# Attention of a streaming-encoder layer: unnormalised softmax with one buffer, against scaled probabilities of two key groups on two column halves

## The reference, cut to what matters

```
s = einsum('bcqhgd,bcshd->bchgqs', qc, kb) * (A_HEAD_DIM ** -0.5)
s = where(valid, s + bias, -1e30)
m = maximum(max(s, axis=-1), sink)
p = exp(s - m)
denom = sum(p, axis=-1) + exp(sink - m)
o = einsum('bchgqs,bcshd->bcqhgd', p / denom, vb)
...
mix = concatenate([y_a, y_b], axis=-1)      # y_a: attention, y_b: retention
x = x + mix @ w_out
```

## Time and profile before

| what | us |
|---|---|
| median of 3 runs (577.29 to 580.09) | 577.47 |
| the profiled execution | 576.34 |
| its span, first to last instruction | 574.2 |
| TensorE busy in it | 549.9 |
| VectorE, ScalarE, GpSimd busy | 423.5, 359.3, 116.7 |

### The profile page before, as it was taken

The page is one execution under the profiler, slowest core; times in us unless marked ns, Lnnn a source line. Parts: engine busy times, 40 slices in busy tenths (PEclk is TensorE's granted clock), DMA queues, the critical chain, the costliest instruction groups (busy, mean ns, idle before and its releaser), DMA issues.

```text
span 574.2 us, 8097 instructions
## 1 busy us (share of the span) xinstructions
PE 549.9 (96%) x2782; PEld 451.3 (79%) x2783; DVE 423.5 (74%) x572; ACT 359.3 (63%) x477; POOL 116.7 (20%) x102
## 2 busy tenths in 40 slices
PE   3999999999999999998999999999999999999992
PEld 3988878888878888876788888888888888888860
DVE  2664577454764843377988889888898888988887
ACT  4563554781134363335778887788877888778823
POOL 3350000000000000002443234432244323411100
PEclk9999999999999999999999999999999999999998
DMA  8989212203020236677999999999999999999173
GB/s 299 373 277 387 58 36 74 74 20 128 1 73 1 74 111 226 231 276 272 344 390 373 371 366 365 368 367 335 346 372 389 372 359 374 369 389 339 34 294 146
DMA packets 72044, 144.32 MB, mean 251 GB/s; under 512 B 3794, under 2 KB 13322, under 8 KB 71888
## 3 DMA queue, kind: packets, MB, share of 16 engines
q1 hardware_dynamic: 65936, 124.96, 61.7%
q0 software_dynamic: 6080, 19.00, 9.5%
HBM read 132.77 MB, written 14.69 MB: 257 GB/s over the span
## 4 chain that ended last, share of the span: by engine, by line
PE 85%; DVE 6%; DMA 4%; issue 2%; ACT 1%; SPq 0%; POOL 0%; POOLq 0%; DVEq 0%
PE ps L1317 24%; PE ps L1319 23%; PE ps L1318 23%; PE ps L1324 6%; PE ps L1429 2%; PE ps L1466 2%; PE ps L1454 2%; DMA arena<-y_dram 1%; PE ps L1497 1%; PE ps L1399 1%; DMA arena<-norm_g 1%; PE ps L1420 1%; DVE res L1304 1%; DMA arena<-h_dram,meta 1%; PE ps L1337 1%
## 5 line engine op out<-in xcount | busy, mean ns | idle before, releaser
L1117 DVE TENSOR_TENSOR lo_ring<-arena,hi_ring 128x2048 fp32r<-128x2048 f32 x94 | 215.1, 2291 | 28.5 <-ACT hi_ring L808 27.4
L1317 PE MATMUL ps<-hi_ring,act_hi 128*128 128x512 f32 x576 | 232.6, 404 | 0.5 <-DVE act_lo L911 0.5
L1319 PE MATMUL ps<-hi_ring,act_lo 128*128 128x512 f32 x576 | 225.2, 391 | 0.0
L1318 PE MATMUL ps<-lo_ring,act_hi 128*128 128x512 f32 x576 | 224.7, 390 | 0.0
L808 ACT ACTIVATE hi_ring<-arena 128x2048 fp32r<-128x2048 f32 x94 | 180.2, 1917 | 18.6 <-PE ps L1319 18.6
L1317 PEld LDWEIGHTS ps<-hi_ring,act_hi 128*128 128x128 f32 x576 | 108.3, 188 | 27.4 <-issue 6.0
L1319 PEld LDWEIGHTS ps<-hi_ring,act_lo 128*128 128x128 f32 x576 | 108.1, 188 | 23.6
L1318 PEld LDWEIGHTS ps<-lo_ring,act_hi 128*128 128x128 f32 x576 | 108.4, 188 | 20.2
L901 DVE SCALAR_TENSOR_TENSOR lo_ring<-arena,over,hi_ring 128x512 fp32r<-128x512 f32 x40 | 29.4, 748 | 33.5 <-ACT hi_ring L640 33.5
L911 DVE TENSOR_TENSOR act_lo<-ps,act_hi 128x512 fp32r<-128x512 f32 x64 | 41.7, 683 | 11.6 <-ACT act_hi L669 5.8
L563 POOL DMA_INDIRECT y_dram<-y,row_info x15 | 16.1, 1073 | 149.6 <-issue 149.6
(11 more groups left out here) (197 smaller groups left out, 564.1 us busy)
## 6 DMA issues: line engine op xcount, KB each, us to landing
arena<-w_gate SPq DMA_DIRECT2D x32, 1024.0 KB, 15.2
arena<-w_up SPq DMA_DIRECT2D x32, 1024.0 KB, 15.8
arena<-w_down SPq DMA_DIRECT2D x32, 1024.0 KB, 15.6
arena<-w_in SPq DMA_DIRECT2D x16, 512.0 KB, 7.8
y_dram<-arena POOLq DMA_DIRECT2D x8, 512.0 KB, 11.8
arena<-w_out SPq DMA_DIRECT2D x4, 1024.0 KB, 5.2
arena<-y_dram SPq DMA_DIRECT2D x8, 512.0 KB, 7.1
arena<-w_in SPq DMA_DIRECT2D x3, 1024.0 KB, 12.9
```

The costliest lines, as they stand in the source:

```text
L1117: nc.vector.tensor_tensor(lo(N1 + n12), raw(n12), hi(N1 + n12).bitcast(F32), ALU.subtract).then_inc(lo_done, 1)
L1317: nc.tensor.matmul(dst, a_hi, b_hi, start=start, stop=False)
L1318: nc.tensor.matmul(dst, a_hi, b_lo, start=False, stop=False)
L1319: return nc.tensor.matmul(dst, a_lo, b_hi, start=False, stop=stop)
```

## The change

- Unit u's probabilities lie in one of two buffers by kv; the second lies in the unused half of `mix`. Their small statistics are doubled too. `zeros`, the source of the clearing of `y_dram`, shrinks to half and is read twice by each transfer.
- `softmax_denom(u)` also multiplies the probabilities by the reciprocal (128x768, or 128x512 for the first tile), and signals `p_scaled`. In VectorE's order it now stands after `softmax_logits` of the same slot, that is of unit u+1.
- `turn_prob(u)` moves from slot 2u+2 to 2u+3, waits for `p_scaled`, and orders its blocks by key block, so that all four heads are side by side in a bank.
- `values(t)` works on both kv of a token tile at once: values are the stationary side (64 columns), the turned probabilities stream as 512 columns, the result is bank 6 with 64 rows for each kv, already turned (head widths as rows, heads and tokens along the free side). It stands in slots 6, 10, 14, 18.
- `attention_out(t)` is a plain copy of 128x512. `turn_mix(0)` is gone; `mix_hi(0)` and `mix_lo(0)` read `mix` and stand in slot 28. The rows of `w_out` for the attention half are loaded in the order of heads, in two transfers to 64 rows each.
- The retention's scores and values, and their masks, move from slots 18, 20 (values 20, 22) to 19, 21 (21, 23); rotations 0 to 3 are turned in bank 4 instead of 7 and wait for the read of the scores.

```diff
 TURN_V_SLOT = 1
-TURN_SLOTS = tuple(range(2, 18, 2))
-SCORE_SLOTS = (0,) + TURN_SLOTS[:-1]
-VALUE_SLOTS = tuple(range(3, 19, 2))
+SCORE_SLOTS = tuple(range(0, 16, 2))
+DENOM_SLOTS = tuple(range(2, 18, 2))
+TURN_SLOTS = tuple(range(3, 19, 2))
+VALUE_SLOTS = tuple(range(6, 22, 4))
 ROTATE_SLOTS = (4, 5, 7, 9, 20, 22, 23, 25)
 ROT_SLOTS = (5, 7, 9, 11, 22, 23, 25, 26)
-ROT_BANKS = (7, 7, 7, 7, 5, 6, 5, 6)
-RET_SCORE_SLOTS = (18, 20, 27, 29)
-MASK_SLOTS = (18, 20, 27, 31)
-RET_VALUE_SLOTS = (20, 22, 31, 32)
+ROT_BANKS = (4, 4, 4, 4, 5, 6, 5, 6)
+RET_SCORE_SLOTS = (19, 21, 27, 29)
+MASK_SLOTS = (19, 21, 27, 31)
+RET_VALUE_SLOTS = (21, 23, 31, 32)
 RET_BANKS = (7, 4, 7, 4)
-MIX_A_SLOT, MIX_B_SLOT = 31, 35
+MIX_A_SLOT, MIX_B_SLOT = 28, 35
 TURN_X2_STEPS = ((N1 - 3, 1), (N1 - 3, 2), (N1 - 3, 3), (N1 - 2, 0), (N1 - 2, 1), (N1 - 2, 2), (N1 - 2, 3))
...
 SCM_OFF = (0, 512, 896, 1152)
+TWO_PART_OUT = (NA + NB, NA + NB + 2)
...
+
+
+def probs_value(u):
+
+    return u + 1 if u < 2 else 2 * u
 def build(nc, x, norm1_g, w_in, attn_sinks, rel_bias, ret_gn_g, w_out, norm2_g, rg_w, rg_b, re_w, re_b,
...
         gn_g = region(O_GN, 512)
-        prob = region(O_P, 1024).rearrange("p (h j) -> p h j", h=4)
-        prob_pairs = region(O_P, 1024).rearrange("p (i a j) -> p a i j", i=2, a=2)
+        prob = [region(O_P, 1024).rearrange("p (i a j) -> p i a j", i=2, a=2),
+                mix[:, 2:4, 512:1024].rearrange("p i (a j) -> p i a j", a=2)]
         bias_pairs = region(O_BIAS, A_HEADS * WIN).rearrange("p (i a j) -> p a i j", i=4, a=2)
-        prob_t = region(O_PT, 1024).rearrange("p (h b q) -> p h b q", h=4, b=2)
+        prob_t = [[region(O_PT, 512), region(O_PT + 512, 512)],
+                  [region(O_MIX + b * D + 512, 512) for b in range(2)]]
         scm = region(O_SCM, 1280)
...
         sum_sq, rms, eps = stat[:, 0:12], stat[:, 12:24], stat[:, 44:46]
-        neg_max, sink_d, p_sum, denom, r_denom = (stat[:, 24 + 4 * i:28 + 4 * i] for i in range(5))
+        neg_max, sink_d, p_sum, denom, r_denom = (
+            [v[:, o + 4 * i:o + 4 * i + 4] for v, o in ((stat, 24), (norm_tmp, 0))] for i in range(5))
         route = y_buf[0][:, 0:640]
...
                     half, cols = (g - NA - NB) % 2, (g - NA - NB) // 2
+                    if half == 0:
+                        for kv in range(2):
+                            sp.dma_start(as_chunks(dst)[kv * A_DIM:(kv + 1) * A_DIM, :, :],
+                                         w_out_heads[:, 4 * kv:4 * kv + 4, 512 * cols:512 * cols + 512]
+                                         ).then_inc(w1_in[slot1(g)], 16)
+                        return
                     src = w_out_v[:, 4 * half:4 * half + 4, 512 * cols:512 * cols + 512]
...
                 elif n == RING1:
-                    sp.wait_ge(m_turned, 2 * T)
+                    sp.wait_ge(m_turned, T)
+                    sp.wait_ge(m_lo, T)
                 elif n == O_P // GRAN:
...
             for b in range(2 * T):
-                pool.dma_start(y_dram[b * P:(b + 1) * P, :], zeros).then_inc(y_zeroed, 16)
-
-            pool.wait_ge(m_turned, 2 * T)
+                pool.dma_start(y_dram[b * P:(b + 1) * P, :].rearrange("p (a n) -> p a n", a=2),
+                               zeros.unsqueeze(1).to_broadcast([P, 2, 512])).then_inc(y_zeroed, 16)
+
+            pool.wait_ge(m_turned, T)
             pool.dma_start(gain2, bass.AP(norm2_g.tensor, 0, [[0, P], [1, D]])).then_inc(gain_in, 16)
...
             def softmax_exp(u):
...
                 act.wait_ge(logit_ready, u + 1)
+                kv = u % 2
                 for hh in range(4):
-                    nc.scalar.activation(prob[:, hh, w0:], prob[:, hh, w0:], ACT.Exp, bias=neg_max[:, hh:hh + 1],
-                                         accum_out=p_sum[:, hh:hh + 1]).then_inc(exp_done, 1)
-                nc.scalar.activation(sink_d, sink_d, ACT.Exp).then_inc(sink_exp, 1)
+                    row = prob[kv][:, hh // 2, hh % 2, w0:]
+                    nc.scalar.activation(row, row, ACT.Exp, bias=neg_max[kv][:, hh:hh + 1],
+                                         accum_out=p_sum[kv][:, hh:hh + 1]).then_inc(exp_done, 1)
+                nc.scalar.activation(sink_d[kv], sink_d[kv], ACT.Exp).then_inc(sink_exp, 1)
             def copy_prob_t(u):
                 act.wait_ge(p_turned, u + 1)
-                b0 = 1 if u < 2 else 0
-                for half in range(2):
-                    v = ps[:, 6 + half, :].rearrange("p (h b q) -> p h b q", h=2, b=2)
-                    nc.scalar.copy(prob_t[:, 2 * half:2 * half + 2, b0:, :], v[:, :, b0:, :]).then_inc(pt_copied, 1)
+                for b in range(1 if u < 2 else 0, 2):
+                    nc.scalar.copy(prob_t[u % 2][b], ps[:, 6 + b, :]).then_inc(pt_copied, 1)
             def copy_rot(n):
...
             def mix_hi(part):
+                if part == 0:
+                    act.wait_ge(mm_done, tile_value(NA + NB - 2, T - 1))
                 for t in range(T):
-                    act.wait_ge(m_turned, T * part + t + 1)
+                    if part:
+                        act.wait_ge(m_turned, t + 1)
+                        rows = ps[:, 4 + t, :]
+                    else:
+                        act.wait_ge(mix_a, t + 1)
+                        rows = mix[:, t, 0:512]
                     nc.scalar.activation(ht_hi[:, 4 * part:4 * part + 4, t * P:(t + 1) * P],
-                                         ps[:, 4 * part + t, :].rearrange("p (k s) -> p k s", k=4),
-                                         ACT.Copy).then_inc(m_hi, 1)
+                                         rows.rearrange("p (k s) -> p k s", k=4), ACT.Copy).then_inc(m_hi, 1)
             def copy_x2(half, t):
...
                 heads = slice(4 * kv, 4 * kv + 4)
-                if u:
-                    dve.wait_ge(p_turned, u)
+                if u >= 2:
+                    dve.wait_ge(p_turned, u - 1)
                 dve.wait_ge(s_ready, u + 1)
...
                     ins = nc.vector.scalar_tensor_tensor(
-                        prob_pairs[:, half, :, CHUNK + j0:], sc[:, :, j0:], A_DIM ** -0.5,
+                        prob[kv][:, :, half, CHUNK + j0:], sc[:, :, j0:], A_DIM ** -0.5,
                         bias_pairs[:, half, 2 * kv:2 * kv + 2, j0:], ALU.mult, ALU.add)
+                    if half == 0:
+                        ins.then_inc(score_read, 1)
                 step_done(ins)
-                step_done(nc.vector.tensor_reduce(neg_max, prob[:, :, CHUNK + j0:], AX_X, ALU.max))
-                step_done(nc.vector.tensor_tensor(neg_max, neg_max, sinks[:, heads], ALU.max))
-                step_done(nc.vector.tensor_scalar(neg_max, neg_max, -1.0, None, ALU.mult))
-                nc.vector.tensor_tensor(sink_d, sinks[:, heads], neg_max, ALU.add).then_inc(logit_ready, 1)
+                top = neg_max[kv]
+                step_done(nc.vector.tensor_reduce(top.rearrange("p (i a) -> p i a", a=2), prob[kv][:, :, :, CHUNK + j0:],
+                                                  AX_X, ALU.max))
+                step_done(nc.vector.tensor_tensor(top, top, sinks[:, heads], ALU.max))
+                step_done(nc.vector.tensor_scalar(top, top, -1.0, None, ALU.mult))
+                nc.vector.tensor_tensor(sink_d[kv], sinks[:, heads], top, ALU.add).then_inc(logit_ready, 1)
             def softmax_denom(u):
...
                 dve.wait_ge(sink_exp, u + 1)
-                step_done(nc.vector.tensor_tensor(denom, p_sum, sink_d, ALU.add))
-                step_done(nc.vector.reciprocal(r_denom, denom))
-
-            def attention_out(u):
-                t, kv = u // 2, u % 2
-                dve.wait_ge(o_ready, u + 1)
-                if u == 2 * (T - 1):
+                kv, w0 = u % 2, P if u < 2 else CHUNK
+                step_done(nc.vector.tensor_tensor(denom[kv], p_sum[kv], sink_d[kv], ALU.add))
+                step_done(nc.vector.reciprocal(r_denom[kv], denom[kv]))
+                rows = prob[kv][:, :, :, w0:]
+                nc.vector.tensor_tensor(rows, rows, r_denom[kv].rearrange("p (i a) -> p i a", a=2).unsqueeze(3)
+                                        .to_broadcast([P, 2, 2, 2 * P - w0]), ALU.mult).then_inc(p_scaled, 1)
+
+            def attention_out(t):
+                dve.wait_ge(o_ready, t + 1)
+                if t == T - 1:
                     dve.wait_ge(y_zeroed, 16 * 2 * T)
-                nc.vector.tensor_tensor(mix[:, t, 256 * kv:256 * kv + 256].rearrange("p (h c) -> p h c", h=4),
-                                        ps[:, 6, 0:256].rearrange("p (h c) -> p h c", h=4),
-                                        r_denom.unsqueeze(2).to_broadcast([P, 4, A_DIM]), ALU.mult).then_inc(mix_a, 1)
+                nc.vector.tensor_copy(mix[:, t, 0:512], ps[:, 6, :]).then_inc(mix_a, 1)
             def rotate(n):
...
             def mix_lo(part):
                 for t in range(T):
-                    row_lo(ht_lo[:, 4 * part:4 * part + 4, t * P:(t + 1) * P], 4 * part + t,
```

(68 more changed lines are left out.)

12 lines of the change are left out of this document (7 added, 5 removed).

## The result

| | median us | range, executions |
|---|---|---|
| kernel before | 577.47 | 575.54 to 580.87, 11 |
| changed kernel | 583.75 | 580.78 to 585.86, 11 |

The ratio is 1.0098, with a 95% interval of 1.0072 to 1.0123: slower, by 5.7 us on 577.47, where 2.9 us were forecast. The profiled execution took 584.27 us, its span is 582.3, so 8.1 us more span than before.

The account below looks back on a forecast made before the run. TensorE was taken to bound the kernel, its work and waits costing their whole length: 6.6 + 11.16 - 14.84 = +2.9 us on 576.34, 579.3; the median lies 1.13 higher, so 580.4 us, range 575.5 to 586.5.

Parts of the forecast that it names:

- the experts' phase is only shifted: After the mixer: the experts' part would start later by the mixer's change and cost nothing more itself.
- at nothing: Mixer: edits priced at zero, such as 7.1 us of VectorE scaling and mix copies moved from slot 31 to 28.
- Value products: TensorE in the mixer: 14 matmuls, 28 records of 512 columns, column halves side by side, adding 6.6 us.
- The row halves of the scores: Scores on TensorE: two records run at once with 0.2 us to enter; the same was taken for column halves.
- The rule weighed against it: Value products: weight loads overlap only across row groups; one exposed 0.19 us load per pair, 2.6 us more, chance 0.08.
- The multiplication: VectorE scaling of probabilities, 128x768 from SBUF to SBUF: taken as 0.96 us, with no row of its own.
- Waits of the units: TensorE before turned probabilities: waits of 0.49, 0.98, five times 1.25 and 0.4 us behind logits, denominator and scaling.
- the step from VectorE to TensorE: From the end of a scaling on VectorE to the start of TensorE's transposes: taken as 0.05 us.
- First rotation: turn_rot(0) on TensorE: a wait of 1.64 us behind unit 1's scaling, for 1.03 before.
- values(2): TensorE at values(2): a 0.45 us wait because ScalarE's silu copies with table loads delay a probability copy.
- Retention rotations: Rotations 5 and 7 behind retention outputs on VectorE: 0.4 + 0.85 less a 0.3 us gap, 0.95 us, bounds 0 and 2.
- turn_mix(0) and the copies moved: 16 transposes removed, 1.75 us saved; their copies and subtractions move from slot 31 to 28, where VectorE and ScalarE have room.

## Why the prediction came out as it did

The direction was right and the mechanism is the one described; the size was too small by 2.8 us on the first measurement and by 0.8 on the second (0.64% of 578.52 is 3.7 us). Two steps of it failed, "the experts' phase is only shifted" and the work moved "at nothing"; the clock was not in it. Point by point, where a cost is counted by the distance of starts, as the prediction counted its waits:

- **Value products**, 6.6 us: 1.0 us for four records and 1.86 for eight make 1.0 + 3 x 1.86 = 6.6. The row halves of the scores were the right row for the cost of column halves. The rule weighed against it fails here: 1.86 us for four pairs is 4 x 0.414 and 0.2 us, which leaves room for one exposed weight load of 0.19 us, not for four. The weight loads of the second pair start at 99.30 us, while the first pair, begun at 99.25, still streams in the same rows. "TensorE: Matmul & The Clock Gate", Part 3, The mechanism, of the Trainium skill has it that a weight load overlaps a product in flight only where the row group differs; that does not hold for these column halves. The same section of the Trainium skill also lets a load into the background weight buffer go ahead of products in flight, which the prediction left out and with which these rows agree.
- **The multiplication**, 0.96 us: measured 0.96. The three widths, 256, 512 and 768 columns at 0.42, 0.69 and 0.96 us, lie on one line.
- **Waits of the units**, 0.49 + 0.98 + 5 x 1.25 + 0.4 = 8.1 us: listed 0.25, 0.96, 4 x 1.22 and 1.23, 0.39, in all 7.7. Each costs 0.15 or 0.16 us more than its listed idle, as shown at 84.17, so some 8.9 us: 0.41, 1.12, five times 1.37 or 1.38, 0.54. This term was short by 0.8 us. The way idle is listed is not the reason, since the 1.25 us was taken between starts as well. The logits took 2.53 us (2.52 predicted), the denominator 0.41 (0.40), the scaling 0.96. What was off is the step from VectorE to TensorE: 0.14 us behind seven of the eight scalings (85.63 to 85.77 in the two timelines above), where 0.05 was taken, as it is behind the rotation; and the tile product covers 2.86 us of the chain and not 2.90. What makes the longer step is not shown.
- **First rotation**, 1.64 in place of 1.03: listed 1.28, so 0.4 less than predicted. **values(2)** behind the table loads, 0.45: 0.33 listed, 0.5 as counted above. **Retention rotations**, 0.95: 0.36 and 0.74 listed, 1.4 as counted above, and 1.1 less the gap of 0.3 before. These two came to 0.2 us more than predicted.
- **turn_mix(0) and the copies moved**, at nothing beyond the 1.75 us removed. This step failed: here a cover was taken away. In slot 31 ScalarE copies v at 191.38 for 0.37 us, when the last product has left PSUM, and the retention values need it; before, the 16 transposes stood between (the row at 184.49 is the turn of that slot). Now TensorE waits 0.51 us, 0.67 as counted above. The prediction asked what hides the moved work, and not what the moved work had hidden.
- **"The experts' phase is only shifted"**: failed. The second turn of the mix begins 5.9 us later than before (201.51 and 207.37), the first expert's turn 5.6 (262.21 and 267.79), the end 8.1. The fall of the clock at 269.4 adds 1.6 us up to the next transposes (272.68 and 279.89), 0.4 of it is taken back where the kernel before waits at 276.77 and the changed one does not, and from there to the last tile products the distance stays at 6.8 us. The last 1.3 us come at the very end, where the last products wait longer for VectorE: 2.9 us in two waits, where the kernel before has the row below. The changed kernel run again had 2.0 us there, so this cost is not fixed; what sets it is not known.

```profile
PE ps L1698 <- DVE res L1304: 1.5, 1, 1.5
```

- **The clock** was no term of the sum at all. The fall at 75 us costs 1.7 us in this execution.

Put together up to the second turn of the mix: 2.9 + 0.8 (units) - 0.4 (rotation) + 0.2 (retention) + 0.7 (slot 31) + 1.7 (clock at 75) = 5.9 us; measured 5.9. Of the 8.1 us some 3 are clock (1.7 at 75 us, 1.2 net at the experts' start). Neither the clock nor the wait at the end was in the sum, so how near the medians come to 2.9 us depends also on how many executions of either kernel had falls; that much of it is luck. The price of the waits has a check of its own in the two profiles compared above: without the fall at 75 us the changed kernel is 7.8 us behind the one with its transposes a slot later, where the listed waits differ by 7.2.

What stays open: what decides whether the clock falls. Every fall inside the kernel, in all ten profiles, follows waits of TensorE: 0.96 and 1.28 us in a row, a single one of 2.6 or 2.7 us, or 0.8 and then 2.0 to 2.5 us at the experts' lists. Part 1 of the same page of the Trainium skill says that the clock follows how busy TensorE has been of late, and the direction agrees. But single waits of 1.2 us, as those of units 2 to 6, were followed by no fall in any profile, and the longer ones not always: 0.95 and 1.27 us with the products half by half, 3.1 us with the denominator first, 2.6 us with the retention output later, and 0.8 and 2.3 us in the first profile of the kernel before passed without one.

## What to carry to other kernels

Where an engine is busy to the last, a shortened operation pays only if its inputs are there: list for each new wait the whole queue ahead of the releasing instruction, on each engine of the chain, and look at moving the consumer before reordering one producer. Reordering VectorE alone took this kernel from 0.6% behind the one before to 1.7%; turning a slot later took it to 0.8% ahead. When work is taken away from a bound engine, ask what other engine's work it was covering. And before a loss of a few us is explained by a fall of the clock, look whether the kernel before has that fall in another of its executions.

## What was not expected of the hardware

- The kernel before has one profiled execution with a fall of TensorE's clock to half for 6.8 us in its middle and one without, though TensorE waits 0.8 and 2.3 us ahead of it in both; the changed kernel's two have 3.4 and 6.8 us there. The two spans of the kernel before are 574.2 and 576.7 us, 2.5 apart, nearly as much as the change was forecast to do.
- Products of one column half each run two at once in f32, in either order of issue: eight records of 512 columns in 1.86 us, where one record alone takes 0.41 to 0.43 us.
- TensorE's transposes started 0.14 us behind the end of the multiplication that released them in seven of eight cases, and 0.05 us behind the end of a rotation.
